# Three convolution layers on x times the norm weights, the norm's factor applied to their products; low halves on GpSimd, VectorE's steps reordered

## What is computed

```python
h = rmsnorm(x, g)                   # x * rsqrt(mean(x*x) + eps) * g
u = causal_dwconv(h @ w_up, w, b)   # per column: three taps along the tokens
a, b = split(u, 2)                  # 2816 columns each
return x + (silu(a) * b) @ w_down
```

## Time and profile before

| | us |
|---|---|
| runs of the kernel | 2141.77, 2159.13, 2171.64 |
| median | 2159.13 |
| span of the profiled execution | 2150.0 |
| TensorE busy | 2122.7 (99%) |
| VectorE, ScalarE, GpSimd busy | 1437.0, 1158.6, 477.9 |
| mean granted TensorE clock | 0.988 |

### The profile page before, as it was taken

One profiled execution on the slowest core, in us unless ns is written; L12 is line 12 of the kernel. 1 busy time (PEld: TensorE's weight loads), 2 busy tenths in 40 slices (PEclk: granted clock), 3 DMA queues, 4 the chain that ended last, 5 costly groups with the idle time before them and its releaser, 6 DMA issues.

```text
span 2150.0 us, 47664 instructions
## 1 busy us (share of the span) xinstructions
PE 2122.7 (99%) x19346; PEld 2057.3 (96%) x19346; DVE 1437.0 (67%) x1972; ACT 1158.6 (54%) x1579; POOL 477.9 (22%) x254
## 2 busy tenths in 40 slices
PE   9999999999999999999999999999999999999998
PEld 8989999999999999988999999997999999999998
DVE  5666888657887899756899766567523454557554
ACT  6624655656666444664544544466544554556565
POOL 0030000100000355131354344310144400001443
PEclk9999999999999999998999999999999999999999
DMA  7223666444675787542788588644355453444552
GB/s 273 86 29 147 234 253 234 161 153 168 250 271 187 289 336 302 213 155 97 272 326 314 214 307 310 243 171 151 138 195 185 174 209 139 154 161 177 190 192 107
DMA packets 64391, 438.95 MB, mean 204 GB/s; under 512 B 7127, under 2 KB 9848, under 8 KB 12170
## 3 DMA queue, kind: packets, MB, share of 16 engines
q1 hardware_dynamic: 60480, 430.75, 54.0%
q10 hardware_dynamic: 3786, 6.38, 1.3%
HBM read 434.49 MB, written 2.62 MB: 203 GB/s over the span
## 4 chain that ended last, share of the span: by engine, by line
PE 91%; DVE 3%; ACT 3%; issue 1%; POOL 1%; DMA 0%; POOLq 0%; DVEq 0%
PE ps L346 25%; PE ps L348 25%; PE ps L347 25%; PE ps L360 1%; PE ps L368 1%; PE ps L362 1%; PE ps L1674 1%; PE ps L491 1%; PE ps L388 1%; ACT w_hi L284 1%; PE ps L390 1%; PE ps L389 1%; POOL hf L475 1%; PE ps L484 1%; PE ps L1696 1%
## 5 line engine op out<-in xcount | busy, mean ns | idle before, releaser
L346 PE MATMUL ps<-h_hi,w_hi 128*128 128x256 f32 x3412 | 956.3, 280 | 2.2 <-DVE h_lo L2442 1.3
L347 PE MATMUL ps<-h_lo,w_hi 128*128 128x256 f32 x3412 | 949.9, 278 | 0.0
L348 PE MATMUL ps<-h_hi,w_lo 128*128 128x256 f32 x3412 | 949.8, 278 | 0.0
L290 DVE TENSOR_TENSOR w_lo<-ring,w_hi 128x2048 fp32r<-128x2048 f32 x272 | 623.7, 2294 | 375.9 <-ACT w_hi L284 371.9
L284 ACT ACTIVATE w_hi<-ring 128x2048 fp32r<-128x2048 f32 x334 | 639.1, 1914 | 147.3 <-PE ps L348 142.7
L346 PEld LDWEIGHTS ps<-h_hi,w_hi 128*128 128x128 f32 x3412 | 644.6, 189 | 9.3 <-issue 6.5
L348 PEld LDWEIGHTS ps<-h_hi,w_lo 128*128 128x128 f32 x3412 | 644.9, 189 | 0.0
L347 PEld LDWEIGHTS ps<-h_lo,w_hi 128*128 128x128 f32 x3412 | 644.0, 189 | 0.2
L346 PE MATMUL ps<-g_hi,w_hi 128*128 (+1 forms) x1232 | 342.1, 278 | 1.6 <-POOL g_lo L894 0.9
L347 PE MATMUL ps<-g_lo,w_hi 128*128 (+1 forms) x1232 | 341.8, 277 | 0.0
L348 PE MATMUL ps<-g_hi,w_lo 128*128 (+1 forms) x1232 | 341.8, 277 | 0.0
(11 more groups left out here) (475 smaller groups left out, 2534.0 us busy)
## 6 DMA issues: line engine op xcount, KB each, us to landing
ring<-in_weights SPq DMA_DIRECT2D x334, 1024.0 KB, 4.8
mix<-in_modw SPq DMA_DIRECT2D x72, 1024.0 KB, 4.8
bias_rows<-below_mix ACTq DMA_DIRECT2D x1, 1536.0 KB
mix<-in_c_ssd ACTq DMA_DIRECT2D x1, 1536.0 KB, 8.1
x<-in_x SPq DMA_DIRECT2D x2, 512.0 KB, 3.8
ring<-in_weights SPq DMA_DIRECT2D x2, 512.0 KB, 6.5
mix<-in_c SPq DMA_DIRECT2D x2, 512.0 KB, 5.6
mix<-bias_rows ACTq DMA_DIRECT2D x1, 1024.0 KB, 8.4
```

What stands on the lines that cost most here:

```text
L290: dve.tensor_tensor(w_lo[:, n % SLOTS], ring[:, n % SLOTS], w_hi[:, n % SLOTS], ALU.subtract).then_inc(lo_ready[n % SLOTS], 1)
L346: pe.matmul(o, w[0], a_hi, start=first, stop=False, **kw)
L347: pe.matmul(o, w[0], a_lo, start=False, stop=False, **kw)
L348: return pe.matmul(o, w[1], a_hi, start=False, stop=last, **kw)
```

## The change

In ffn0, ffn1 and ffn6 (`scaled`) h_hi and h_lo are made of x times the norm weight, without the factor. TensorE starts units 0 and 1 with their products with h_hi, then sums the squares (GpSimd has added them to two tiles), does the h_lo products of unit 0, spreads the factor, and does those of unit 1. ScalarE copies the factor to SBUF. VectorE multiplies each up bank by the factor into `zs`, which frees the bank; ScalarE makes `acc` from `zs`. In ffn1 TensorE first waits for the last residual, in ffn6 the tiles are taken in another order (2 and 3 late). ffn0 and ffn1 now run with GpSimd making g_lo and the low halves of the down weights (`dve_alone` and `dve_glo` are empty). VectorE's order becomes: even m: factor, products, taps; odd m: factor, gate of m-1, low half of the even weights, taps, low half, gate of m. Ahead of these stages both halves of `lo_half` stand before the second residual. At the end of the program 48 matmuls without use (`last_products`) stand for two of `keep_warm`. (Branches for "dil" in `scaled` are not reached.)

```diff
-        dve_alone = ("ffn0", "ffn1")
+        dve_alone = ()
+        dve_glo = ()
+        scaled = ("ffn0", "ffn1", "ffn6")
...
+        def scaled_act(act, tag, eps, gain, prev_last):
+            for q, (k, n) in enumerate(square_tiles(tag, KD)):
+                act.wait_ge(*after(f"dve:{STAGES[STAGES.index(tag) - 1]}.res{q}"))
+                for b in range(k, k + n) if tag != "ffn6" or q not in (1, 3) else () if q == 1 else (6, 2, 3):
...
+                    act.activation(h_hi[:, b], x[:, b], ACT.Copy, scale=gain(b)).then_inc(*step(f"act:{tag}.hi{b}"))
+                act.activation(hf[:, k:k + n], x[:, k:k + n], ACT.Square).then_inc(*step(f"act:{tag}.sq{q}"))
...
+        def scaled_units(pe, tag, n):
+            if tag == "ffn1":
+                pe.wait_ge(*after("dve:dil.res4"))
+            for u in range(2):
...
+                for k in scaled_order(tag, KD):
...
+            scaled_pe_sums(pe, tag)
+            for u in range(2):
+                for k in range(KD):
...
+                        done = pe.matmul(o, w_hi[:, (n + u) % SLOTS, c:c + P], h_lo[:, k], start=False,
...
+                done.then_inc(unit_done, 1)
+                if u == 0:
+                    norm_pe_over(pe, tag)
...
+        def last_products(pe):
+            flat = h_hi[:].rearrange("p k t -> p (k t)")
+            for o in (8, 24, 40, 56, 4, 12, 20, 2):
+                for j in range(6):
+                    pe.matmul(ps[1][:, 0:T], w_hi[:, 0, P * j:P * j + P], flat[:, T * j + o:T * j + o + T], start=True, stop=True)
...
+                late = STAGES[STAGES.index(tag) + 1] in scaled
+                if between is not None and q == (0 if late and tag.startswith("ffn") else 1):
                     lo_half(dve, between, 0)
+                    if late:
+                        lo_half(dve, between, 1)
...
+                if name in scaled:
+                    if m == 0:
+                        act.wait_ge(unit_done, n + 1)
+                        hi(act, n + SLOTS)
+                    act.wait_ge(z_free, zbase[name] + m + 1 + i * 2)
...
+                        src = zs[:, e, half] if name in scaled else ps[e][:, half * T:(half + 1) * T]
+                        done = act.activation(acc[:, e, half], src, ACT.Identity,
...
+                        dve.wait_ge(unit_done, n + 1 + i * 3)
+                        dve.tensor_tensor(zs[:, e], ps[e][:].rearrange("p (a b) -> p a b", a=2), by_block(rstd[:], 2),
+                                          ALU.mult).then_inc(z_free, 1)
+                        if m == 0:
+                            lo(dve, n + SLOTS)
+                        if m % 2 == 0:
+                            products(m, i)
+                        else:
+                            gate(m - 1, i)
+                            if m > 1:
+                                lo(dve, n - 1 + SLOTS, i)
+                        dve.wait_ge(acc_done, 22 * scaled_convs.index(name) + m + 1 + i * 2)
...
+                if name in scaled:
+                    if m % 2 == 1:
+                        if m < KF - 1:
+                            lo(dve, n + SLOTS, i)
+                        gate(m, i)
+                    return
...
             def down(j, n, i):
-                if j < 9:
+                if j < 9 and name not in dve_alone:
                     lo(pool, n + SLOTS, i)
```

More of the change, by code:

```diff
@@ L355, in a_unit @@
             if parts:
-                for k in range(ks):
+                for k in scaled_order(parts, ks):
                     pe.wait_ge(*after(f"act:{parts}.hi{k}"))
@@ new lines, in scaled_pool @@
+        def scaled_pool(pool, tag):
+            for name, a, b, waits in (("pair0", 0, 1, ("act:{}.sq0",)), ("pair1", 2, 3, ("act:{}.sq1",)),
+                                      ("quad", 0, 2, ("pool:{}.pair0", "pool:{}.pair1")), ("pair2", 4, 5, ("act:{}.sq2",)),
+                                      ("six", 0, 4, ("pool:{}.quad", "pool:{}.pair2")), ("pair3", 6, 7, ("act:{}.sq3", "act:{}.sq4"))):
+                for w in waits:
+                    pool.wait_ge(*after(w.format(tag)))
+                pool.tensor_tensor(hf[:, a], hf[:, a], hf[:, b], ALU.add).then_inc(*step(f"pool:{tag}.{name}"))
@@ new lines, in scaled_pe_sums @@
+        def scaled_pe_sums(pe, tag):
+            for k, w in ((0, "six"), (6, "pair3")):
+                pe.wait_ge(*after(f"pool:{tag}.{w}"))
+                done = token_sums(pe, ps[6], k, lambda c: slice(c, c + 1), ones[:, 0:1], int(k == 0), k == 6)
+            done.then_inc(*step(f"pe:{tag}.ss"))
+        def scaled_units(pe, tag, n):
+            if tag == "ffn1":
+                pe.wait_ge(*after("dve:dil.res4"))
+            for u in range(2):
+                pe.wait_ge(lo_ready[(n + u) % SLOTS], (n + u) // SLOTS + 1)
+                for k in scaled_order(tag, KD):
+                    if u == 0:
+                        pe.wait_ge(*after(f"act:{tag}.hi{k}"))
+                    for b in range(2):
+                        c, o = (2 * k + b) * P, ps[u][:, b * T:(b + 1) * T]
+                        pe.matmul(o, w_hi[:, (n + u) % SLOTS, c:c + P], h_hi[:, k], start=b == 0 and k == 0, stop=False,
+                                  skip_group_check=True)
+                        pe.matmul(o, w_lo[:, (n + u) % SLOTS, c:c + P], h_hi[:, k], start=False, stop=False,
+                                  skip_group_check=True)
+            scaled_pe_sums(pe, tag)
+            for u in range(2):
+                for k in range(KD):
+                    if u == 0 and k % 2 == 0:
+                        pe.wait_ge(*after(f"dve:{tag}.lo{k // 2}"))
+                    for b in range(2):
+                        c, o = (2 * k + b) * P, ps[u][:, b * T:(b + 1) * T]
+                        done = pe.matmul(o, w_hi[:, (n + u) % SLOTS, c:c + P], h_lo[:, k], start=False,
+                                         stop=b == 1 and k == KD - 1, skip_group_check=True)
+                done.then_inc(unit_done, 1)
+                if u == 0:
+                    norm_pe_over(pe, tag)
@@ L429, in square_tiles, with scaled_dve @@
+        def scaled_dve(dve, tag, gain):
+            for q in range(4):
+                for b in (2 * q, 2 * q + 1):
+                    dve.wait_ge(*after(f"act:{tag}.hi{b}"))
+                    done = dve.scalar_tensor_tensor(out=h_lo[:, b], in0=x[:, b], scalar=gain(b), in1=h_hi[:, b],
+                                                    op0=ALU.mult, op1=ALU.subtract)
+                done.then_inc(*step(f"dve:{tag}.lo{q}"))
         def square_tiles(tag, kb):
@@ L622, in residual_dve @@
                 done.then_inc(*step(f"dve:{tag}.res{q}"))
-            if between is not None:
+            if between is not None and not late:
                 lo_half(dve, between, 1)
@@ L1835, in dil_act @@
                 act.wait_ge(unit_done, b + l + 1)
+                if "dil" in scaled:
+                    if what == "v":
+                        act.wait_ge(z_free, zbase["qkv"] + l)
+                        for c in range(NCH):
+                            done = act.activation(dl_v[:, c, 256 * j:256 * j + 256], ps[l % 2][:, c * T:(c + 1) * T], ACT.Copy,
+                                                  scale=rtok[:, c:c + 1])
+                        done.then_inc(z_free, 1)
+                    hi(act, b + l + SLOTS)
+                    continue
                 if what == "v":
```

107 lines of the change are left out of this document (88 added, 19 removed).

## The result

| | before | after |
|---|---|---|
| median of 6 runs, us | 2156.2 | 2209.2 |
| lowest to highest | 2141.8 to 2171.6 | 2206.9 to 2220.2 |
| span of the profiled execution | 2150.0 | 2207.4 |
| mean granted clock | 0.988 | 0.988 |

The ratio is 1.027, with a 95% interval from 1.023 to 1.030: the changed kernel is 53 us slower; 2212 was predicted. The page of after has this where the earlier trace rows stand: TensorE is busy for 97% of the span, and VectorE and GpSimd are busy 85 and 149 us longer.

A forecast was written before the change was run, and what follows sets the result against it. TensorE, busy 99% of 2150.0 us, was taken as the bound. ffn0 +23.2, ffn1 +30.3 and ffn6 +2.0 made +55.5, a span of 2205; 53 added to the median 2159.1 gave 2212 us, range 2165 to 2240.

The forecast's parts named there:

- The ring: Loops of ffn0 and ffn1: products held behind GpSimd's low half close a cycle of 19.3 us per turn; chance 0.49.
- The two ends of a stage: Waits of TensorE: 3.0 or 2.6 us ahead of down(0), 3.3 to 3.5 ahead of down(10).
- D: Rival: stalls in ffn0 and ffn1 also lower TensorE's clock, 1.7 us each, +27, 2239 us; chance 0.17.
- The norm: Head of ffn0, ffn1 and ffn6: it leaves TensorE's path, gaining 3.0, 1.9 and 4.2 us, together 9.1.
- I charge no wait: Start of a stage: ScalarE makes each h_hi in about 0.4 us, TensorE spends 0.47 on each, so no wait.
- ffn6: Stage without products: waits at its ends and 0.9 us in the loop, +6.2, less 4.2 for the norm: +2.0.
- changes only where TensorE has stood still: TensorE's loops: matmul pace, 117.6 or 113.4 ns, shifts only after a standstill; a stage differs by 7 us.
- No wait above 0.1: Loop of ffn6: TensorE should show no wait longer than 0.1 us.
- The tail: End of the program: 48 matmuls replacing 2 cost zero, up to 5 us if they ran at half clock.
- B: Rival: products not held or slip in ahead of GpSimd, only waits at stage ends stay, +11, 2170 us; chance 0.16.
- C: Rival: all stalls are hidden and the norm's 9.1 us are won, 2150 us; chance 0.13.
- E: Rival: no stalls, and the three stages all run at the fast pace, 2125 us; chance 0.05.

The follow-up runs named there:

- x5: Changed kernel with GpSimd making each low half of a down weight twice in ffn0 and ffn1: median 2286.9 us, 1.056 of the kernel before.
- x8: Changed kernel with both GpSimd jobs back on VectorE in ffn0 and ffn1, new order kept: median 2177.1 us, 1.009 of the kernel before.
- y3: Changed kernel with ffn0 and ffn1 as before, only ffn6 and the end changed, measured a second time: 1.005 of the kernel before.
- x3: Changed kernel with ffn0 and ffn1 as before, only ffn6 and the end changed: median 2153.3 us, 0.997 of the kernel before.

## Why the prediction held, step by step

**The ring.** With P as the end of GpSimd's low half (631.64 in the turn shown):

| step ends | predicted | measured |
|---|---|---|
| taps of the even unit begin | P + 2.8 | 2.9 |
| factor of the odd unit | 5.1 | 5.2 |
| low half of the even weights | 7.7 | 7.9 |
| g_lo | 8.3 | 8.5 |
| taps of the odd unit | 9.7 | 9.9 |
| low half | 11.9 | 12.1 |
| w_hi on ScalarE | 14.7 | 14.8 |
| GpSimd's next low half | 19.3 | 19.5 |

From the matmul before it, the even up unit starts 2.0 to 2.2 us later (a wait of about 2 was predicted) and the down unit 0.55 to 0.98 (0.3 to 0.8). The premise under it, that the products are held and the factor's multiplication from PSUM is not, is in the rows at 256 us. What remains open is small: the links add up 0.2 us too short.

**The two ends of a stage** were sized too large. Ahead of down(0) I had 3.0 or 2.6 us: it was 1.4 in ffn0 and ffn6 and 2.4 in ffn1. In ffn0 a wait of 2.1 in the first turn followed as predicted, in ffn1 none in the first turn and 1.4 ahead of the second (at 581.0), for the 2.8 that I had in the first. Ahead of down(10) it was 2.2 (ffn0, ffn6) and 3.1 (ffn1) for 3.3 to 3.5. That is 2.3 us less for ffn0 than I summed up, and it still grew by 25.9 us where 23.2 were predicted. Against it stand 0.2 us in each turn of the ring (1.6), the norm (0.8, below) and the clock (some 3, under D): errors that offset each other. So the closeness of the total is in part luck: the three stages grew by 62.6 us and not by 55.5, and only the 5.2 us won elsewhere brought the span (2207.4) so near the 2205 of the sum.

**The norm** gained 7.7 us, not 9.1. The stretch from the last matmul of the stage before to unit 2, the first three stages in order:

```profile
196.77:209.94 13.17, 13.06 (x119) 12.40 (x118) 9.82 (x14) 8.16 (x15) 3.96 (x5) 1.00 0.64 241
528.65:542.08 13.43, 12.58 (x119) 12.37 (x119) 9.52 (x14) 9.09 (x15) 4.12 (x5) 1.00 0.43 155
2006.91:2019.91 13.00, 12.87 (x119) 12.40 (x118) 8.93 (x14) 9.39 (x16) 4.07 (x5) 1.00 0.37 133
```

Two units of 5.44 us are in it, so the norm costs 2.3, 2.6 and 2.1 now; the earlier trace rows, from last matmul to unit 1, less one unit, gave 4.3, 4.35 and 5.6, and read from the same start as here 4.5, 4.5 and 5.7. The gains are 2.2, 1.9 and 3.6 for 3.0, 1.9 and 4.2. The step that failed is "I charge no wait": while h_hi tiles arrive, some matmuls of ffn0 and ffn6 start 0.2 to 0.4 us after the one before instead of 0.11, the largest distance being 0.39 in ffn0 and 0.41 in ffn6; in ffn0 these waits add up to the missing 0.8.

**ffn6** came out at +5.1 where +2.0 was summed up. Waits grew by 2.8 us (1.4, 0.6, 2.2 less 1.1 and some) where I had 6.2, the norm gave 3.6, and the pace took 5.9: 1487 matmuls at 117.4 ns instead of 113.4. The sentence that failed is that the pace "changes only where TensorE has stood still" and so averages out. It does change there, but a loop that stalls by a hair when fast and not when slow keeps drawing until it is slow, as far as the traces go: why a stall is followed by one pace or the other is open. "No wait above 0.1" was the right forecast of the size, and the wrong idea of what such a wait can cost.

**The tail** cost next to nothing: from the last product to the end pass 9.0 us before (2140.97 to 2150.0) and 9.3 after (2198.15 to 2207.4). The 48 matmuls run 5.95 us from 2201.22.

**The rivals.** B (products not held) falls with their rows of 4.7 us; C and E (all hidden) with TensorE's 22 to 24 us of waiting in each stage. D (the clock falls at the stalls) came true in a small part. Behind 6 of the 35 or so stalls of ffn0 and ffn1 some 15 matmuls run at 213 ns, at the lower level of 1.2 GHz, which costs 1.5 us. Stretches of after: behind the stall of the last turn in ffn0, behind down(10)'s wait there, and behind a stall of the same length in ffn1, where the clock stays.

```profile
386.00:390.00 4.00, 4.00 (x22) 4.00 (x23) 4.00 (x6) 1.27 (x2) 0.30 (x1) 0.57 0.81 262
...
407.00:412.00 5.00, 5.00 (x33) 5.00 (x33) 2.51 (x3) 4.15 (x5) 0.99 (x1) 0.69 0.02 3
...
639.80:641.00 1.20, 1.20 (x12) 1.20 (x12) 1.20 (x3) 0.85 (x1) 0.29 (x1) 1.00 0.86 109
```

In x5 it happens behind every stall of 5.6 us:

```profile
664.40:666.00 1.60, 1.60 (x8) 1.60 (x9) 1.10 (x4) 0.00 (x0) 0.00 (x0) 0.50 0.38 67
```

Yet its turn is 23.9 us with nothing for the clock: 19.5, and the 5.6 by which GpSimd's two instructions (653.74 to 663.91) outlast the one of 4.62, less the 1.2 of the product that now ends between them. So D's working had a wrong step: it added the clock's price to the ring, but where a ring sets the turn, a slower TensorE only waits less afterwards. Only the falls behind the last stalls of a stage, with no turn to come, are paid: about 3 us in ffn0 and 1.1 in ffn1.

## What to carry to other kernels

Before work goes from a full engine to an idle one, write down what each of the two holds up in the other, and follow one turn around until it closes: if the sum of the links is above what the bounding engine needs, each microsecond in any link costs one per turn, though the idle engine is at 28%. A long instruction of GpSimd beside a VectorE instruction with two SBUF inputs counts in full, through the hold: 4.6 us instead of VectorE's own 2.3 made the turn 2.2 us longer, although the two engines work side by side. And when a change shortens the path of a norm by 2 us, price the order that it forces on the loop behind it: here it cost 12 us a stage without any GpSimd work (x8), through a ring of its own.

## What the runs showed of the hardware that I had not expected

TensorE has two exact paces for the same stream of 128x256 matmuls at a granted clock of 1.00. In the 13 traces, the 52 stages ffn2 to ffn5 last 173.97 us 42 times and 180.79 us 10 times, with nothing between: 113.3 and 117.8 ns per matmul. The pace changes where TensorE has been held up and nowhere else: of 244 stalls of over 0.3 us between two products (L346 to L348 before, L350 to L352 in the others) 188 were followed by the fast pace, 124 of 164 that came after it and 64 of 80 that came after the slow one. So the pace before tells nothing. The delay can be very small: at 1982.40 in y3, where the next matmul comes 0.13 us later instead of 0.12, the slow pace ends. What decides it stays open; no run here tried it. For one stage it is worth 6.8 us, more than the norm gained in any of the three. It is a part of what tells equal runs apart, but how much isn't shown, as each kernel has one trace: x3 and y3, one kernel, have spans 12.8 us apart (2151.7 and 2138.9), and 6.4 of it is ffn1, slow in the one and fast in the other.

The second surprise is how little work a hold needs: the 64-column product, 0.21 us long, took 4.20.
